# The seam between the last cached sequence and the output projection: weight splits moved to later pages, the first mixture transposed in page 15, the second behind the value products

## The reference

```python
h = rms_norm(x, norm_mix); z = h @ w_in                  # q latent | kv latent | rotary key | conv input
attn = attend(...)                                       # prompt: causal; sample: 16 cached pages per sequence + itself
conv = silu(layer_norm(depthwise_conv(glu(u))))          # 512 channels, width 31
mix = concat(rms_norm(attn, norm_out_attn), rms_norm(conv, norm_out_conv))   # width 1024
x = x + mix @ w_out                                      # the output projection
h = rms_norm(x, norm_ffn)
x = x + (silu(h @ w_gate) * (h @ w_up)) @ w_down
x = x + sigmoid(rms_norm(x, norm_ple) @ w_ple_gate) * (pe @ w_ple_proj)
```

## Time and profile before

| | |
|---|---|
| median of 3 runs | 1705.98 us (1704.33 to 1709.04) |
| the profiled execution | 1708.97 us |
| its span, first to last instruction | 1706.7 us |
| mean granted clock of PE | 0.994 |
| busy: PE, PEld (weight load), DVE, ACT, POOL | 97%, 87%, 73%, 39%, 31% |

### The profile page before, as it was taken

How to read it: one execution, slowest core, us unless ns; L and a number is a source line. 1 busy time by engine, 2 the same in 40 slices (tenths; PEclk the granted TensorE clock), 3 DMA queues, 4 the chain that set the end, 5 groups by cost and what they waited for, 6 DMA issues and landing times.

```text
span 1706.7 us, 29004 instructions
## 1 busy us (share of the span) xinstructions
PE 1656.3 (97%) x10698; PEld 1487.6 (87%) x10698; DVE 1244.2 (73%) x1843; ACT 660.3 (39%) x1240; POOL 527.2 (31%) x353
## 2 busy tenths in 40 slices
PE   8999899999999999989999999999999999999998
PEld 8999787676899888877889999999999888888886
DVE  5386886777899999866698777777777577955444
ACT  5303255664544444554443232222232234542111
POOL 2204695420566556531125222222221000700000
PEclk9999999999999999999999999999999999999999
DMA  6401000002252222330104444444444877662111
GB/s 194 145 1 49 15 1 0 2 1 55 51 166 59 58 59 57 87 105 1 50 26 144 144 143 143 143 143 143 143 143 150 303 246 261 200 219 80 42 35 46
DMA packets 156044, 172.89 MB, mean 101 GB/s; under 512 B 35155, under 2 KB 107376, under 8 KB 155805
## 3 DMA queue, kind: packets, MB, share of 16 engines
q1 hardware_dynamic: 153939, 170.52, 31.2%
q10 hardware_dynamic: 2002, 1.03, 0.2%
HBM read 131.06 MB, written 40.80 MB: 101 GB/s over the span
## 4 chain that ended last, share of the span: by engine, by line
PE 77%; DVE 9%; POOL 5%; issue 3%; SPq 2%; ACT 2%; DMA 1%; POOLq 0%; DVEq 0%; ACTq 0%
PE ps L2626 21%; PE ps L2628 21%; PE ps L2627 21%; POOL stats L984 3%; PE ps L3061 2%; PE ps L2858 1%; PE ps L624 1%; PE ps L2948 1%; PE ps L2885 1%; DVE arena L2192 1%; POOL arena L1027 1%; SPq L769 1%; PE ps L2838 1%; PE ps L2632 1%; PE ps L2633 1%
## 5 line engine op out<-in xcount | busy, mean ns | idle before, releaser
L1134 POOL TENSOR_TENSOR arena<-arena,mhalf 128x32 f32<-128x32 f32 x32 | 176.2, 5507 | 121.0 <-DVE arena L2196 121.0
L2626 PE MATMUL ps<-cw_hi,pT_hi 128*128 128x288 f32 x512 | 164.7, 322 | 2.7 <-DVE pT_lo L2084 1.7
L1798 DVE SCALAR_TENSOR_TENSOR arena<-arena,tapw 128x1024 f32<-128x1024 f32 x120 | 162.4, 1353 | 1.9
L2400 DVE TENSOR_TENSOR dn_lo<-dn_raw,dn_hi 128x1024 fp32r<-128x1024 f32 x83 | 115.9, 1407 | 59.9 <-ACT dn_hi L1701 58.9
L2626 PE MATMUL ps<-T_hi,S_hi 128*128 128x272 f32 x528 | 152.7, 289 | 3.7 <-DVE F_B_r L678 1.8
L2627 PE MATMUL ps<-F_B_r,S_hi 128*128 128x272 f32 x528 | 152.3, 288 | 0.0
L2628 PE MATMUL ps<-T_hi,S_lo 128*128 128x272 f32 x528 | 151.9, 288 | 0.0
L2627 PE MATMUL ps<-cw_lo,pT_hi 128*128 128x288 f32 x512 | 151.2, 295 | 0.0
L2628 PE MATMUL ps<-cw_hi,pT_lo 128*128 128x288 f32 x512 | 151.1, 295 | 0.0
L1701 ACT ACTIVATE dn_hi<-dn_raw 128x1024 fp32r<-128x1024 f32 x83 | 87.6, 1060 | 130.7 <-DMA dn_raw<-wt_mid 62.0
L1449 ACT ACTIVATE arena<-ps 128x512 f32<-128x512 f32 x128 | 76.7, 599 | 117.6 <-PE ps L2628 116.6
(11 more groups left out here) (407 smaller groups left out, 4871.1 us busy)
## 6 DMA issues: line engine op xcount, KB each, us to landing
dn_raw<-act_mid SPq DMA_DIRECT2D x77, 256.0 KB, 2.8
arena<-in_cache_ckv SPq DMA_DIRECT2D x128, 128.0 KB, 2.1
dn_raw<-in_w_down SPq DMA_DIRECT2D x45, 256.0 KB, 3.7
w_raw<-in_w_gate SPq DMA_DIRECT2D x22, 512.0 KB, 4.1
w_raw<-in_w_up SPq DMA_DIRECT2D x22, 512.0 KB, 5.3
arena<-in_w_down SPq DMA_DIRECT2D x22, 512.0 KB, 5.6
act_mid<-arena SPq DMA_DIRECT2D x11, 1024.0 KB, 7.5
wt_mid<-arena SPq DMA_DIRECT2D x11, 1024.0 KB, 4.3
```

The lines of the kernel that those rows point to most:

```text
L1134: nc.gpsimd.tensor_tensor(rstd_k[:, 4 * q:4 * q + 4, :], ms_k[:, 4 * q:4 * q + 4, :], mhalf[:, 0:4 * NH].rearrange("p (g h) -> p g h", h=N ...
L1798: ins = nc.vector.scalar_tensor_tensor(y_of(c), glu[:, c, k:k + SEQ], tapw[:, c, k:k + 1], y_of(c), ALU.mult, ALU.add)
L2400: nc.vector.tensor_tensor(dn_lo_r[s], dn_raw[s], dn_hi[s][0], ALU.subtract).then_inc(s_("a_split"), 1)
L2626: mm(out, left[0], right[0], start=start, stop=False)
```

## The change

- Weight blocks 0, 1, 6, 7, 2 are split in pages 4, 6, 8, 9, 9 instead of 0, 1, 4, 7, 8 (blocks 3 and 4 stay in 10 and 12).
- The first tile is normed earlier: `centre` in page 6 (was 9) and `centred_square` in page 7 (was 10); `variance` in 7 (was 10); `layer_norm` in 9 (was 11); `conv_silu` in 10 (was 12); `mix_stat` in 11 (was 13); `mix_scale` in 13 (was 15). POOL's `mix_pool` goes ahead of its power for pages 8 to 11.
- `m_T(0)` goes ahead of page 15's products on PE, `high_m(0)` ahead of page 15's squares on ACT, and `low_m(0)` ahead of its sums on DVE.
- Behind the pages, `layer_norm(1)`, `conv_silu(1)`, `mix_stat(1)` and `mix_scale(1)` go ahead of steps of the softmax; the Exp of one element moves from ahead of `high_m(0)` to just ahead of `soft_exp(7)`.
- `m_T(1)` goes ahead of `lat_T(7)`, directly behind the value products.

No arithmetic, no shape and no transfer changes.

```diff
--- before.py
+++ after.py
@@ -108,7 +108,7 @@
 SEQ_TILES = [TILES] + list(range(TILES))
 OUT_TILES = [7, 6, 0, 1, 2, 3, 4, 5, TILES]
 PLE_TILES = [2, 3, 4, 5, 0, 1, 6, TILES, 7]
-WO_PAGE = dict(zip(WO_ORDER, (0, 1, 4, 7, 8, 10, 12)))
+WO_PAGE = dict(zip(WO_ORDER, (4, 6, 8, 9, 9, 10, 12)))
 
 F32 = mybir.dt.float32
 F32R = mybir.dt.float32r
@@ -1137,7 +1137,6 @@
                         low_q(b + 1)
                     if b == NSEQ - 1 and q == 1:
                         ln_pool(1, P)
-                    if b == NSEQ - 1 and q == 2:
                         mix_pool(1, P)
             ln_pool(2, P)
             mix_pool(2, P)
@@ -1507,6 +1506,9 @@
                     n = NPAGE * b + g
                     if g % 2 == 0 and n // 2 + 1 < NPAGE * NSEQ // 2:
                         high_pair(n // 2 + 1)
+                    if b == NSEQ - 1 and g == NPAGE - 1:
+                        high_m(0, 0)
+                        high_m(0, 1)
                     page_square(b, g)
                     if b == 0 and g in (0, 1):
 
@@ -1518,11 +1520,11 @@
                     if g % 4 == 1 and n >= 4:
                         kpe_copy(b if g > 1 else b - 1, g // 4 - 1 if g > 1 else 3)
                     if b == NSEQ - 1:
-                        if g in WO_PAGE.values():
-                            high_wo([k for k in WO_PAGE if WO_PAGE[k] == g][0])
+                        for k in (k for k in WO_PAGE if WO_PAGE[k] == g):
+                            high_wo(k)
+                        if g == 7:
+                            centred_square(0)
                         if g == 10:
-                            centred_square(0)
-                        if g == 12:
                             conv_silu(0)
                     if g == 2 and 1 <= b < NSEQ - 1:
 
@@ -1545,13 +1547,11 @@
                     chunk_copy(1 + CHUNK_AFTER.index(b))
 
             kpe_copy(NSEQ - 1, 3)
-            nc.scalar.activation(unit_out[:, 2:3], ident[0:1, 0:1], ACT.Exp)
-            high_m(0, 0)
-            high_m(0, 1)
             high_wo(5)
             centred_square(1)
+            conv_silu(1)
+            nc.scalar.activation(unit_out[:, 2:3], ident[0:1, 0:1], ACT.Exp)
             soft_exp(NSEQ - 1, 1)
-            conv_silu(1)
             for j in range(1, NT):
                 high_m(j, 0)
                 if j == 1:
@@ -2187,7 +2187,8 @@
                     if g == 15:
                         quad(b, s, 2)
                         if b == NSEQ - 1:
-                            mix_scale(0)
+                            low_m(0, 0)
+                            low_m(0, 1)
                     dve.wait_ge(s_("ksq_ready"), NPAGE * b + g + 1)
                     nc.vector.reduce_sum(ms_k[:, g, :], ksq[g % 2].rearrange("p (h d) -> p h d", d=DN), AXX)\
                         .then_inc(s_("ksum_done"), 1)
@@ -2207,16 +2208,18 @@
                         shift(b - 1, 1 - s)
                     taps((TAP_PAGES if prev else FIRST_TAP_PAGES).count(g))
                     if b == NSEQ - 1:
-                        if g in WO_PAGE.values():
-                            low_wo([k for k in WO_PAGE if WO_PAGE[k] == g][0])
+                        for k in (k for k in WO_PAGE if WO_PAGE[k] == g):
+                            low_wo(k)
+                        if g == 6:
+                            centre(0)
+                        if g == 7:
+                            variance(0)
                         if g == 9:
-                            centre(0)
-                        if g == 10:
-                            variance(0)
+                            layer_norm(0)
                         if g == 11:
-                            layer_norm(0)
+                            mix_stat(0)
                         if g == 13:
-                            mix_stat(0)
+                            mix_scale(0)
                     if prev and g == 12:
                         out_lat(b - 1, 1 - s)
                     if b >= 2 and g == 0:
@@ -2229,18 +2232,16 @@
 
             out_latT(NSEQ - 2, 0)
             max_three(NSEQ - 1, 1)
-            low_m(0, 0)
-            low_m(0, 1)
             centre(1)
             low_wo(5)
             variance(1)
             last_quad(NSEQ - 1, 1)
+            layer_norm(1)
             row_of_max(NSEQ - 1, 1)
+            mix_stat(1)
             shift(NSEQ - 1, 1)
-            layer_norm(1)
-            mix_stat(1)
+            mix_scale(1)
             out_lat(NSEQ - 1, 1)
-            mix_scale(1)
             out_latT(NSEQ - 1, 1)
             for j in range(1, NT):
                 low_m(j, 0)
@@ -3022,6 +3023,8 @@
                     n = NPAGE * b + g
                     if g % 2 == 0 and n // 2 + 1 < NPAGE * NSEQ // 2:
                         pair_T(n // 2 + 1)
+                    if b == NSEQ - 1 and g == NPAGE - 1:
+                        m_T(0)
                     page_K(b, g)
                     if g % 4 == 2 and n >= 4:
                         kpe_scores(b if g > 2 else b - 1, g // 4 - 1 if g > 2 else 3)
@@ -3080,7 +3083,6 @@
                     chunk_T(b, 1 + CHUNK_AFTER.index(b))
             pe.wait_ge(s_("sc_used"), 4 * NSEQ - 1)
             kpe_T(NSEQ - 1, 3)
-            m_T(0)
             kpe_scores(NSEQ - 1, 3)
             pe.wait_ge(s_("ksq_ready"), NPAGE * NSEQ)
             wout(0, range(0, 5))
@@ -3089,8 +3091,8 @@
             max_B(NSEQ - 1)
             wout(0, range(6, KC))
             pv(NSEQ - 1, 1)
+            m_T(1)
             lat_T(NSEQ - 1)
-            m_T(1)
             pe.wait_ge(s_("olT_ready"), NSEQ)
             for h in range(NH):
                 for k in range(LC):
```

## The result

| | before | changed |
|---|---|---|
| median | 1705.98 us | 1713.83 us (9 runs, 1710.53 to 1714.09) |
| ratio, changed to before | | 1.0035, 95% interval 1.0026 to 1.0044 |
| profiled execution, span, clock | 1708.97, 1706.7, 0.994 | 1714.02, 1711.8, 0.992 |

The change makes the kernel slower by 0.35%, 4.4 to 7.5 us, 6.0 in the middle (the two medians lie 7.85 us apart). Forecast were +3.9 us and 1709.9 us. The median, 1713.83 us, is inside the upper end of the range (1714.0) by 0.17 us, and two of the nine executions lie above it: that the range held was luck. "Within 0.3%" had the larger chance and did not come; rival 1 (slower, by the clock, +7.3) came nearer.

What follows compares the result with a forecast made beforehand. PE bounds the kernel, busy 97% of the span, so only its idle time and clock count. Terms of +2.2 us plus +1.7 for the clock gave +3.9, from 1705.98 to 1709.9 us; range 1704.5 to 1714.0.

Steps and rivals of the forecast that it cites:

- Within 0.3%: Whole kernel: the measured time cannot be told from no change, 0.3% being 5.1 us; chance 0.67.
- rival 1: Three long standstills each lead to a 1.2 GHz stretch on PE's path, the old one stays: +7.3, 1713.3 us; chance 0.25.
- to `pv(6)`: splits gone, squares ahead of the exponentials: Pages 0 to 8: `max_T(6)` wait shrinks by 1.1, but squares wait for DVE's `centre`; path 1.3 us late.
- `pv(6)` to `wout(0)`: Pages 10 to 15: 18.4 instead of 19.5 us, -1.1; about 3 us wait for `mix_scale(0)`, none ahead of `wout(0)`.
- `wout(0)` to `pv(7)`: Page 15's sum comes later, PE waits 1.1 us at `max_T(7)`, `shift(7)` is held 0.4: +1.5 us.
- `pv(7)` to `wout(1)`: `m_T(1)` ahead of `lat_T(7)` fills the 1.50 us wait for `out_lat`, `olT_ready` uncovered for 0.5: -0.8 us.
- `wout(1)` to `m_T(2)`: The silu table load falls to `conv_silu(2)` and goes onto the path in full: +1.3 us.
- clock: Slow stretches at 1.2 GHz on PE's path, 1.7 us each: +1.7 us, bounds -1.7 and +5.1.
- The mechanism said to speak against the change: `centred_square(0)` in page 7: ACT stands 2 us for DVE's `centre(0)`, so `pv(6)` waits 3.7 us.
- The price of 1.28 us for the table load: Silu table load ahead of `m_T(2)` costs 1.28 us; a drain of about 1.38 us on top was left out.
- two stretches on the path more and one less: Behind waits at `pv(6)`, `m_T(0)`, `m_T(2)` two slow stretches come, the one behind `pv(7)` goes, 1.7 us each: +1.7.
- From `wout(2)` on PE goes without a gap: Behind the changed places PE never waits, so nothing there gives the delay back.

Runs made afterwards that it cites:

- f3: Changed kernel with spare PE products that nothing reads ahead of `pv(6)`, `m_T(0)` and `m_T(2)`; 1709.75 us, +2.0 us to the kernel before.
- e4: Kernel before with only the new pages of the weight-block splits; 1707.80 us, -0.7 us to the kernel before.
- f1: Changed kernel timed and profiled once more, nothing edited; 1713.47 us, +6.5 us to the kernel before.
- e1: Changed kernel with the first tile's squares behind the exponentials in page 8 on ACT, variance in page 8; 1709.34 us, +0.9 us to the kernel before.
- e2: Changed kernel with a one-element Silu right behind the last exponentials, loading the table there; 1710.88 us, +2.2 us to the kernel before.
- h1: Changed kernel with spare PE products ahead of `pv(6)` and `m_T(0)` only; 1711.11 us, +0.7 us to the kernel before.
- g2: Changed kernel with squares and variance in page 8, silu table early, `lat_T(7)` ahead of `m_T(1)` again; 1706.77 us, -1.4 us to the kernel before.

## Why the prediction was right, and where it was short

f3 is the changed kernel with no slow stretch, so its distances carry the terms of the sum alone, and the kernel before is what they are held against, or e4 in the last two rows before the sum, where the former had a slow stretch. The direction and most shifts, stretch by stretch, came as forecast; that the total fell inside the range was luck, as said above.

| term of the sum | forecast | measured |
|---|---|---|
| to `pv(6)`: splits gone, squares ahead of the exponentials | +1.3 | +1.36 (25.75 - 24.39) |
| `pv(6)` to `wout(0)` | -1.1 | -1.15 (22.44 - 23.59) |
| `wout(0)` to `pv(7)` | +1.5 | +0.86 (13.30 - 12.44) |
| `pv(7)` to `wout(1)` | -0.8 | -0.77 (8.74 - 9.51 in e4) |
| `wout(1)` to `m_T(2)` | +1.3 | +1.20 (8.73 - 7.53 in e4) |
| sum without the clock | +2.2 | +1.50 |
| clock | +1.7 | about +4 |

The second row is held against the kernel before, as the forecast did it, and its 23.59 us include that kernel's slow stretch behind page 14's wait. Against e4, which had none (23.10), the term is -0.66 and the sum +2.0. The medians agree with either: what is left of a difference in time when the difference in the column of the clock is taken off is 6.0 - 4.4 = 1.6 us for the changed kernel and 6.5 - 4.3 = 2.2 for f1.

- **The order** was predicted well. The mechanism said to speak against the change was the one that did: e1 removes it and with it most of the loss. `m_T(0)` came 14.4 us behind the end of `pv(6)` in f3, with 14.5 forecast, but PE's idle time on the way lay at three places (1.20, 0.42 and 2.30 us) and not at one of 3. The largest miss is `max_T(7)`, where PE waited 0.54 us in f3 and 0.32 in the changed kernel, not 1.1.
- **The price of 1.28 us for the table load** was right (e2: 2.87 to 1.59). The Trainium skill (ScalarE: Activation LUTs, What ACT_TABLE_LOAD costs) has a drain of about 1.38 us on top. The trace does not agree: with the load moved away the wait shrank by 1.28, not 2.7.
- **The step that was mis-sized is the clock**, "two stretches on the path more and one less". In the profiled execution 5.65 us (91.08 - 85.43 in f3) were lost in the seam against 1.56 before (11.07 - 9.51 from `pv(7)` to `wout(1)`) plus at most 0.5 at page 15 (23.59 - 23.10); that is +3.6 by the sum of +2.0, or +4.1 by the one of +1.5. Over all runs the loss is 12.8 and 13.0 us instead of 8.4 and 8.7, so +4.4. Three things were off. The three long standstills were given two stretches, and each of them had one in the first profile, two of them in f1's. Both old stretches went, not one; the one behind page 14's wait had cost at most 0.5 us, and going it is part of the -1.1 above. And the one behind `m_T(2)` cost 2.8 us in the one profile (1.6 in f1 and h1). The 1.7 us for one stretch, which the windows shown with the prediction (1.2 and 1.5 us) don't give, held elsewhere: 1.69 us at `pv(6)`, 1.45 at `m_T(0)` (5.48 us to `wout(0)`, 4.03 in f3). Rival 1 had +5.1 for the clock, and the +6.0 measured lie beyond the +5.6 from which it was to decide; it was right that all three places lead to a stretch, and wrong that the old one stays.
- **"From `wout(2)` on PE goes without a gap"** was wrong. It stands for 1.84 to 1.86 us between 866 and 880 us in every version, with further waits behind. In the profile of the kernel before the clock stayed up there; in the changed kernel it fell. The row ahead and the window behind, changed kernel:

```profile
877.37 0.37 PE L2627 MATMUL ps<-B_hi,A_hi 128*128 128x272 f32 x1 [1.84 <-issue]
```

```profile
878.00:882.00 4.00, 4.00 (x21) 3.92 (x20) 3.97 (x6) 1.09 (x3) 0.00 (x0) 0.57 0.02 4
```

## What to carry to other kernels

Ahead of putting a step into an idle place of a helper engine, look at what is queued behind it there: here two squares in front of the exponentials on ACT cost PE 2.6 us (`pv(6)` at 25.73 us, 23.15 in e1; moving the splits hid half of it), and the slow clock behind the longer wait another 1.7. A function-table load belongs where its engine is idle ahead of the input, not between the input and the function; a one-element activation puts it there. Where a change lengthens a standstill of PE past those behind which the clock already falls in the trace, count a slow stretch for each such place, and take several profiles before a price is put on one.

## What the runs showed of the hardware

Whether the granted clock falls behind a standstill is not settled by its length, though the longest were followed by a fall most often. Over the fourteen profiles of this study (unfilled waits of the seam, and the one near 875 us; the length of one kernel's wait is nearly the same in each):

| standstill | clock fell behind it |
|---|---|
| 3.75 us, `pv(6)` | 4 of 4 |
| 2.87, `m_T(2)` | 3 of 4 |
| 2.30, `m_T(0)` | 5 of 7 |
| 1.63 and 2.11, `wout(0)` (kernel before, e4) | 0 of 2 |
| 1.85, near 875 us | 9 of 14 |
| 1.74 and 1.75, page 14 (kernel before, e4) | 1 of 2 |
| 1.59 to 1.68, `m_T(2)` | 0 of 7 |
| 1.50, `lat_T(7)` (kernel before, e4, g2) | 1 of 3 |
| 1.14 to 1.26, `pv(6)` | 0 of 7 |

The same kernel, changed and f1, had it fall behind 2.30 us in one execution and not in the other. Most lengths occur at one place only, so what the length does and what the work ahead of it does are not told apart here. The Trainium skill (TensorE: Matmul & The Clock Gate, Part 1) says that idleness takes the clock down; these rows agree, but show that one standstill of given length does not settle it. Single profiles of one kernel differ by it: `m_T(3)` lay 91.1 us behind the mark in the changed kernel's and 88.7 in f1's.
